# The last two experts in another order: both ups ahead of both downs, with the turns and the rows inside the downs

## The reference

```
h = rmsnorm(x, g);  proj = h @ w_in                 # q, k, v, pooling input, gates
... pooling branch, attention branch ...
x = x + merged @ w_out
h2 = rmsnorm(x, ffn_g)
logits = h2 @ router_w + router_b;  top_v, top_i = lax.top_k(logits, 4);  top_p = softmax(top_v)
for e in range(32):
    g = min(t @ w_gate[e] + b_gate[e], 7)
    u = clip(t @ w_up[e] + b_up[e], -7, 7)
    act = (u + 1) * (g * sigmoid(1.702 * g))
    out = out + comb[:, e:e+1] * (act @ w_down[e] + b_down[e])
```

## Time and profile before

| | us |
|---|---|
| runs | 1078.42, 1079.12, 1079.86 |
| median | 1079.12 |
| profiled execution, its own time | 1078.32 |
| its span | 1076.0 |
| TensorE busy | 1046.0 (97%) |
| VectorE busy | 272.9 (25%) |
| ScalarE busy | 199.7 (19%) |
| DMA | 433.65 MB, mean 403 GB/s |

### The profile page before, as it was taken

One profiled execution on the slowest core, in us unless ns is written; L12 is line 12 of the kernel. 1 busy time (PEld: TensorE's weight loads), 2 busy tenths in 40 slices (PEclk: granted clock), 3 DMA queues, 4 the chain that ended last, 5 costly groups with the idle time before them and its releaser, 6 DMA issues.

```text
span 1076.0 us, 12286 instructions
## 1 busy us (share of the span) xinstructions
PE 1046.0 (97%) x5121; PEld 445.2 (41%) x5121; DVE 272.9 (25%) x548; ACT 199.7 (19%) x348; POOL 40.4 (4%) x55
## 2 busy tenths in 40 slices
PE   9999999999999999999999999999999999999997
PEld 5899984333333333333333333333333333333332
DVE  6876753111111111111111111111111011111121
ACT  4667522111111101111111111111111011111011
POOL 0460020000000000000000000000000000000000
PEclk9999999999999999999999999999999999999999
DMA  9835999999999999999999999999999999999997
GB/s 313 307 124 163 406 392 378 409 426 428 440 427 431 429 432 432 432 431 434 429 431 432 432 434 430 432 431 430 434 434 430 432 431 430 425 429 429 429 421 282
DMA packets 37947, 433.65 MB, mean 403 GB/s; under 512 B 5109, under 2 KB 7962, under 8 KB 20122
## 3 DMA queue, kind: packets, MB, share of 16 engines
q1 hardware_dynamic: 37280, 432.64, 95.9%
q10 hardware_dynamic: 634, 0.56, 0.2%
HBM read 432.14 MB, written 1.05 MB: 403 GB/s over the span
## 4 chain that ended last, share of the span: by engine, by line
PE 70%; DMA 25%; ACT 3%; DVE 1%; issue 0%; DVEq 0%
PE ps L1063 45%; DMA ring<-in_exp_w_up 22%; PE ps L951 4%; PE ps L691 4%; PE ps L692 4%; PE ps L693 4%; DMA arena<-in_exp_w_up 3%; PE ps L1011 3%; ACT arena L1382 2%; PE ps L1000 1%; PE ps L1071 1%; PE ps L757 1%; PE ps L819 0%; PE ps L968 0%; PE ps L705 0%; ACT ring_r L1244 0%
## 5 line engine op out<-in xcount | busy, mean ns | idle before, releaser
L1063 PE MATMUL ps<-ring,arena 128*64 128x512 f32 x2432 | 543.3, 599 | 12.4 <-DMA ring<-in_exp_w_up 12.1
L1063 PEld LDWEIGHTS ps<-ring,arena 128*64 128x64 f32 x2432 | 168.2, 137 | 337.0 <-issue 313.5
L1063 PE MATMUL ps<-arena 128*64 128x512 f32 x640 | 142.0, 595 | 2.1 <-DMA arena<-in_exp_w_up 1.9
L1880 DVE TENSOR_SCALAR arena<-ps 128x512 f32<-128x512 f32 x30 | 20.8, 692 | 464.4 <-PE ps L1063 464.4
L1382 ACT COPY arena<-ps 128x512 f32<-128x512 f32 x31 | 32.5, 1048 | 255.9 <-PE ps L951 255.9
L1063 PEld LDWEIGHTS ps<-arena 128*64 128x64 f32 x640 | 44.0, 137 | 86.5 <-issue 81.5
L1893 DVE TENSOR_SCALAR arena<-ps 128x512 f32<-128x512 f32 x31 | 21.4, 692 | 177.2 <-PE ps L1063 177.2
L1011 PE MATMUL ps<-arena 64*128 64x512 f32 x256 | 63.9, 616 | 0.0
L1422 ACT COPY arena<-ps 128x256 f32<-128x256 f32 x30 | 11.2, 372 | 279.3 <-PE ps L1011 279.3
L691 PE MATMUL ps<-ring_r 128*128 128x256 f32 (+1 forms) x192 | 59.1, 308 | 0.4 <-DVE arena_r L1682 0.3
L951 PE MATMUL ps<-arena 128*64 128x512 f32 x248 | 58.5, 592 | 0.0
(11 more groups left out here) (245 smaller groups left out, 673.0 us busy)
## 6 DMA issues: line engine op xcount, KB each, us to landing
ring<-in_exp_w_up SPq DMA_DIRECT2D x19, 4096.0 KB, 31.9
ring<-in_exp_w_down SPq DMA_DIRECT2D x18, 4096.0 KB, 31.3
ring<-in_exp_w_gate SPq DMA_DIRECT2D x18, 4096.0 KB, 32.5
ring<-in_exp_w_up SPq DMA_DIRECT2D x10, 2048.0 KB, 39.6
ring<-in_exp_w_down SPq DMA_DIRECT2D x10, 2048.0 KB, 38.9
ring<-in_exp_w_gate SPq DMA_DIRECT2D x10, 2048.0 KB, 40.3
arena<-in_exp_w_gate SPq DMA_DIRECT2D x5, 4096.0 KB, 32.5
arena<-in_exp_w_down SPq DMA_DIRECT2D x5, 4096.0 KB, 34.0
```

What stands on the lines that cost most here:

```text
L1063: last = mm(ps[BLOCK * to:BLOCK * (to + 1), bank, :], src[:, c, half, :], moved, start=(fresh and half == 0 and c == 0), stop=(half == 1 a ...
L1880: v.tensor_scalar(g1, ps[:, 4, :], LIMIT, None, ALU.min).then_inc(g_ready, 1)
```

## The change

Four things move.

The order of the last six matrices is now gate 30, up 30, gate 31, up 31, down 30, down 31, for the loads as for the products. Up 31 and down 30 are both loaded in four pieces of two chunks (up 31 had five, the last two of one chunk). The weights of the last rows are turned inside up 31, ahead of chunk 4. Expert 31's activation is turned inside down 30, ahead of chunks 3 and 5, and the rows of expert 30 are put back inside down 31, ahead of chunks 3 and 5. Down 31 goes to bank 5, since bank 7 is still being read.

The turn of the parameters and the spread of the norms are now two functions; the spread stands ahead of chunk 6 of the first query strip.

The second tile's `pick` for the first expert no longer reads `rank_tab`. It compares the sums in the accumulator directly, and is weighted with `chosen` times the norm; `rank` follows behind it.

```diff
-        GATE30, UP30, GATE31, DOWN30, UP31, DOWN31 = range(PAIR, PAIR + 6)
-        TAIL = {DOWN30: (0, 2, 4, 6, 8), UP31: (0, 2, 4, 6, 7, 8), DOWN31: (0, 2, 4, 6, 7, 8)}
+        GATE30, UP30, GATE31, UP31, DOWN30, DOWN31 = range(PAIR, PAIR + 6)
+        TAIL = {UP31: (0, 2, 4, 6, 8), DOWN30: (0, 2, 4, 6, 8), DOWN31: (0, 2, 4, 6, 7, 8)}
...
-            def spread_norm():
+            def turn_columns():
                 pe.wait_ge(rows_in, 16 * 4)
                 tr(ps[:, 1, R_BGATE:R_ROWS], prow[R_BGATE:R_ROWS, :],
                    ident[R_BGATE:R_ROWS, R_BGATE:R_ROWS]).then_inc(cols_T, 1)
+
+            def spread_norm():
                 pe.wait_ge(con_rest, 16)
...
                                 turn_x(1, 1)
+                                turn_columns()
+                            if t == 0 and c == 6:
                                 spread_norm()
...
-                product(r, 0, DOWN30, 7, actT, fresh=True)
-                pe.wait_ge(weights_ready, r + 1)
-                turn_weights(6)
...
                 pe.wait_ge(pickT_ready, i + 2)
                 biases(1, 5, next_e)
-                product(r, 0, UP31, 5, last_h_in)
-
-                pe.wait_ge(y_ready, i + 2)
-                scatter_tile(0, y_e, pickT)
-                pe.wait_ge(act_first, r + 1)
-                turn_part(0, 4).then_inc(turn_first, 1)
-                scatter_tile(1, y_e, pickT).then_inc(rows_down, 1)
-                pe.wait_ge(act_ready, i + 2)
-                pe.wait_ge(pickT_ready, i + 3)
-                turn_part(1, 6).then_inc(act_T, 1)
+                product(r, 0, UP31, 5, last_h_in, [(4, last_weights)])
+                pe.wait_ge(actT_ready, i + 1)
+                product(r, 0, DOWN30, 7, actT, [(3, first_turn), (5, second_turn)], fresh=True)
                 pe.wait_ge(actT_first, r + 1)
-
-                def rows_turned():
-                    pe.wait_ge(actT_ready, i + 2)
-
-                product(r, 0, DOWN31, 7, last_actT, [(2, rows_turned)], fresh=True)
+                product(r, 0, DOWN31, 5, last_actT, [(2, rows_turned), (3, first_rows), (5, second_rows)], fresh=True)
...
             dve.wait_ge(chosen_ready, 2)
+            own(v.tensor_tensor(first_weight, chosen[:, 1, 0:1], rstd[:, 1:2], ALU.mult))
             dve.wait_ge(rank_done, 2)
+            v.tensor_scalar(pick[:, 1, :], iota, ps[:, 2, 0:1], first_weight, ALU.is_equal, ALU.mult).then_inc(first_pick, 1)
             rank(1)
-            select_tile(1, 0).then_inc(first_pick, 1)
```

More of the change, by code:

```diff
@@ L248, in build @@
         ss_more = small[:, 186:187]
+        first_weight = small[:, 187:188]
         ss2 = small[:, 196:200].rearrange("p (t h) -> p t h", t=NT)
@@ L270, in build @@
         down30_in = [sem(f"down30_in{i}") for i in range(2)]
-        up31_in = [sem(f"up31_in{i}") for i in range(3)]
+        up31_in = [sem(f"up31_in{i}") for i in range(2)]
         down31_in = [sem(f"down31_in{i}") for i in range(5)]
@@ L473, in build @@
         FINE = E - 5
-        GATE30, UP30, GATE31, DOWN30, UP31, DOWN31 = range(PAIR, PAIR + 6)
-        TAIL = {DOWN30: (0, 2, 4, 6, 8), UP31: (0, 2, 4, 6, 7, 8), DOWN31: (0, 2, 4, 6, 7, 8)}
-        TAIL_IN = {DOWN30: [quarter_in[DOWN30 % HOLDS][0], down30_in[0], quarter_in[DOWN30 % HOLDS][1], down30_in[1]],
-                   UP31: [quarter_in[UP31 % HOLDS][0], up31_in[0], quarter_in[UP31 % HOLDS][1], up31_in[1], up31_in[2]],
-                   DOWN31: down31_in}
+        GATE30, UP30, GATE31, UP31, DOWN30, DOWN31 = range(PAIR, PAIR + 6)
+        TAIL = {UP31: (0, 2, 4, 6, 8), DOWN30: (0, 2, 4, 6, 8), DOWN31: (0, 2, 4, 6, 7, 8)}
+        TAIL_IN = {n: [quarter_in[n % HOLDS][0], seconds[0], quarter_in[n % HOLDS][1], seconds[1]]
+                   for n, seconds in ((UP31, up31_in), (DOWN30, down30_in))}
+        TAIL_IN[DOWN31] = down31_in
         def tail_count(signal, r):
@@ L495, in matrix @@
                 return divmod(n, MATRICES)
-            return ((E - 2, 0), (E - 2, 1), (E - 1, 0), (E - 2, 2), (E - 1, 1), (E - 1, 2))[n - PAIR]
+            return ((E - 2, 0), (E - 2, 1), (E - 1, 0), (E - 1, 1), (E - 2, 2), (E - 1, 2))[n - PAIR]
         h_split = tuple(ring_r[seat[H_SLOT]][:, NC * S * i:NC * S * (i + 1)].rearrange("p (c s) -> p c s", c=NC)
@@ L1147, in last_pair, with last_weights, first_turn, second_turn @@
                 product(r, 0, GATE31, 4, last_h_in, [(3, lambda: turn_results(i))])
-                pe.wait_ge(actT_ready, i + 1)
-                product(r, 0, DOWN30, 7, actT, fresh=True)
-                pe.wait_ge(weights_ready, r + 1)
-                turn_weights(6)
+                def last_weights():
+                    pe.wait_ge(weights_ready, r + 1)
+                    turn_weights(6)
+                def first_turn():
+                    pe.wait_ge(act_first, r + 1)
+                    turn_part(0, 4).then_inc(turn_first, 1)
+                def second_turn():
+                    pe.wait_ge(act_ready, i + 2)
+                    pe.wait_ge(pickT_ready, i + 3)
+                    turn_part(1, 6).then_inc(act_T, 1)
+                def first_rows():
+                    pe.wait_ge(y_ready, i + 2)
+                    scatter_tile(0, y_e, pickT)
+                def second_rows():
+                    scatter_tile(1, y_e, pickT).then_inc(rows_down, 1)
+                def rows_turned():
+                    pe.wait_ge(actT_ready, i + 2)
                 pe.wait_ge(pickT_ready, i + 2)
                 biases(1, 5, next_e)
-                product(r, 0, UP31, 5, last_h_in)
-                pe.wait_ge(y_ready, i + 2)
-                scatter_tile(0, y_e, pickT)
-                pe.wait_ge(act_first, r + 1)
-                turn_part(0, 4).then_inc(turn_first, 1)
-                scatter_tile(1, y_e, pickT).then_inc(rows_down, 1)
-                pe.wait_ge(act_ready, i + 2)
-                pe.wait_ge(pickT_ready, i + 3)
-                turn_part(1, 6).then_inc(act_T, 1)
+                product(r, 0, UP31, 5, last_h_in, [(4, last_weights)])
+                pe.wait_ge(actT_ready, i + 1)
+                product(r, 0, DOWN30, 7, actT, [(3, first_turn), (5, second_turn)], fresh=True)
                 pe.wait_ge(actT_first, r + 1)
-                def rows_turned():
-                    pe.wait_ge(actT_ready, i + 2)
-                product(r, 0, DOWN31, 7, last_actT, [(2, rows_turned)], fresh=True)
+                product(r, 0, DOWN31, 5, last_actT, [(2, rows_turned), (3, first_rows), (5, second_rows)], fresh=True)
                 def last_scatter(t, q):
@@ L1439, in last_pair @@
                 fn(sig, g1, ACT.Sigmoid, scale=ALPHA).then_inc(sig_ready, 1)
-                act.wait_ge(piece_done, pieces + 2 * (DOWN30 + 1))
-                nc.scalar.copy(y_e, ps[:, 7, :]).then_inc(y_ready, 1)
                 act.wait_ge(pick_T, i + 2)
@@ L1448, in last_pair @@
                 nc.scalar.copy(turned[:, 2 * P:], ps[:, 6, 2 * P:]).then_inc(actT_ready, 1)
+                act.wait_ge(piece_done, pieces + 2 * (DOWN30 + 1))
+                nc.scalar.copy(y_e, ps[:, 7, :]).then_inc(y_ready, 1)
                 act.wait_ge(piece_done, pieces + 2 * (DOWN31 + 1))
-                nc.scalar.copy(last_y[:, 0:HALF // 2], ps[:, 7, 0:HALF // 2]).then_inc(y_first, 1)
-                nc.scalar.copy(last_y[:, HALF // 2:], ps[:, 7, HALF // 2:]).then_inc(y_ready, 1)
+                nc.scalar.copy(last_y[:, 0:HALF // 2], ps[:, 5, 0:HALF // 2]).then_inc(y_first, 1)
+                nc.scalar.copy(last_y[:, HALF // 2:], ps[:, 5, HALF // 2:]).then_inc(y_ready, 1)
             def experts(r):
```

## The result

| | before | after |
|---|---|---|
| median us (runs) | 1078.95 (20) | 1080.13 (20) |
| lowest to highest | 1077.83 to 1080.78 | 1079.33 to 1081.77 |
| ratio, 95% interval | | 1.0013 [1.0007, 1.0018] |
| profiled execution: own time, span | 1078.32, 1076.0 | 1080.27, 1078.0 |

The change costs 1.4 us by the ratio (0.8 to 1.9 by the interval); the two medians are 1.2 apart. The forecast was 1080.3.

What follows compares the result with a forecast made beforehand. The weight stream was taken to set the end from about 700 us; tail +1.6, second pick -0.2 and spread 0 gave +1.4 us, set on the mean 1078.93: 1080.3 us, range for the time 1078.3 to 1081.6.

Steps and rivals of the forecast that it cites:

- The bound: From about 700 us the weight stream sets the kernel's end; work saved on TensorE comes back as longer waits.
- The tail, +1.6: Last down waits for pieces at 1059.6 and 1062.1, then 7.57 us of chunks and rows stand uncovered: 1.6 us later.
- The second pick, -0.2: Front, second tile: pick ready 0.23 us earlier, two keepers hold TensorE until about 169.8; -0.2 us, bounds -0.2 and 0.
- The spread of the norms, 0: Front: VectorE waits 0.75 us longer, but key strips hang on ScalarE's square; 0 us, bounds 0 and +0.75.
- (d): Front: VectorE's 0.75 us from the later spread pass into the front, giving 1081.1 us; chance 0.07.
- The sum: Whole kernel: +1.6 - 0.2 + 0 = +1.4 us, set on the mean 1078.93, giving 1080.3; chance 0.50.
- One of its signs of being wrong: End of stream: the prediction is wrong if the last landing moves by over 0.3 us against the first product.
- (a): Tail: landings don't bite and the last down runs through; tail -0.16 to +0.1, giving 1078.7 us; chance 0.27.
- (b): Tail: TensorE's waits are the price and landings follow the consumer; -1.7 - 0.2, giving 1077.0 us; chance 0.05.
- (c): Tail: the clock falls after a wait, behind 1062.1 where nothing covers it; 1.7 us on top, 1082.0; chance 0.11.

Runs made afterwards that it cites:

- e5: Kernel before with five more clock keepers (matmuls of no use) ahead of gate 30, where a wait for a landing follows; 1079.03 us, ratio 1.0002.
- e6: Kernel before with five more clock keepers ahead of down 31, where no wait is left; 1080.20 us, ratio 1.0012.
- e1: Kernel after with the old spread of the norms and the old pick, so the tail's change alone; 1080.21 us, ratio 1.0013.
- e3: Kernel after without the two tiles of rows of expert 30 inside the last down, leaving them out of the output; 1078.51 us, ratio 0.9992.
- e8: Kernel after with one clock keeper instead of two between the rank's sums and the second gather; one execution, 1081.55 us.
- e9: Kernel before with one clock keeper instead of two behind the counts of the ranks; one execution, 1078.92 us.
- e2: Kernel before with the late spread of the norms and the early second pick, so the front's change alone; 1078.67 us, ratio 0.9995.
- e4: Kernel after with down 31 loaded in six pieces, so that chunk 2 needs only half of the second; 1079.81 us, ratio 1.0008.
- e7: Kernel before with expert 30's rows moved into up 31, ahead of chunks 2 and 4; 1079.64 us, ratio 1.0005.

## Why the prediction was right, point by point

**The bound.** Right. The share stayed at 1.00 up to 1000 us, and e5 shows that 1.3 us of work on TensorE at 1014 us, ahead of waits, is free (1.0002), while e6 shows that behind the last wait it is paid in full.

**The tail, +1.6.** Right, by its own steps. The first piece was to land at 1059.6 and the second at 1062.1; in e1 it was 1059.33 and 1061.81, after 1060.08 and 1062.57, e3 1060.85 and 1063.33. The distance of 2.49 held in all of them (2.48, 2.49, 2.48), which is what the interpolation rested on; the level moves with the stream. Behind the second piece I had 7.57 us, counted as the old product was with 6.86; its row ends 0.23 later (7.09), so 7.80 to the end of the row. Measured 7.78. On the common measure the tail costs 1.62. That the rows are the uncovered work is shown by e3 (1.74 back in the trace, 1.7 in the time).

**The second pick, -0.2.** Wrong, and this is the step: "two clock keepers from 169.35 hold TensorE until about 169.8". A pair of keepers holds it until 0.67 us behind its start, 169.95 in the profile after: I had taken 0.23 for each of the two starts (0.73 less 0.50), but the gather behind the second one comes later than a second keeper does behind the first. In the earlier trace rows the gather at 170.01 follows the pick's end at 169.93 so closely that VectorE looked like the only cause. With one keeper (e8) the gather starts 0.44 us behind it and 0.07 behind the comparison's end, so there it follows the pick, as in e9, and the pick's 0.22 us show. The price of the scalar from the accumulator is now measured: 0.32 us against 0.31, and the old form took 0.32 too in e9.

**The spread of the norms, 0.** Right in its effect, off in one size: VectorE waits 1.14 us, not 0.75, and starts 1.0 later. The spread itself starts at 14.00, 1.86 later than the 12.14 of the earlier trace rows, where I had reckoned with two chunks of 0.86 and VectorE at 14.5. The slack of ScalarE's path held it, as said, and rival (d) fell: the key strips are not later, and e2 is not slower.

**The sum.** 1080.3 stood for +1.6 and -0.2; the runs gave 1080.13. By the terms as measured it would be +1.6 on the mean of 1078.93, 1080.5. That the median is 0.4 under this is inside the interval (0.8 to 1.9). So the mechanism and the size of the tail were right, but that the forecast came within 0.2 us is in part luck: the 0.2 wrongly taken off for the pick happens to make up half of those 0.4.

**One of its signs of being wrong came.** The prediction called itself wrong if the last landing moved by over 0.3 us against the first product. It did: in the trace's record of the landings it comes 894.15 us behind it in the kernel before and 894.62 after, 0.47 later, and the second piece of the last but one matrix moved alike, from 879.34 to 879.78. The change's order is not needed for that: in e1, with the same order of loads, the second piece comes after 879.06, earlier than before. The limit of 0.3 was narrower than the stream's scatter, so the sign could not tell anything. For the same reason the last down ends 2.08 us later from the start of the span and not 1.4: the stream's shift is some 0.4 of it.

**The rivals.** (a), landings that don't bite, fell: every trace of the new order has its waits inside down 31. (b) fell: the old waits were filled and the time rose, while the landings kept their distances (the last one 14.85 us behind the second piece before and 14.88 after, by the record of the landings). (c) did not occur in the changed kernel's profiled execution nor in e1, e3, e4 or e8. Its event is real, as e7 shows, and there it stood where nothing covered it; the longest wait of the changed kernel's tail on a matmul row is 0.64 us, and in e7 it was 1.17 and 0.46 close together. That is one case and no rule. Only one execution of each kernel has a trace: six of the changed kernel's 20 times lie from 1081.02 to 1081.77, and whether such a product or a late landing made them is not known. (d) fell as told. As to the section "Optimization Strategies" of "Perfetto Trace Analysis" in the Trainium skill, by which the matmul engine is to be kept going: here the change did the turns beside the waits of down 30 and lost, and e6 against e5 shows that what counts is what stands behind the last landing.

No kernel here is faster than the kernel before by more than can be told; e2's 0.9995 [0.9986, 1.0004] is the lowest that computes the whole output.

## What to carry to other kernels

Where a stream of loads sets the end, find the last landing that the program waits for, and add up the work that stands behind it: here only that was paid (e5 against e6). Small work (rows, turns) costs nothing ahead of the last waits only if it uncovers nothing elsewhere: e7 put the rows there and uncovered VectorE's activation. The new order with the rows in the two waits of down 31 was not run, so whether it could have been saved is not shown. Before pricing an earlier result at a gain, list everything that holds its consumer, on the consumer's own engine too; two holders that end together look like one in a trace.

## What the hardware showed that was not expected

- The stream's landings near the end moved between 1051.80 and 1053.60 us for the same transfer over the profiled executions, while the distances behind it stayed: down 31's first piece to its second is 2.49 within 0.02, and the last landing lies 14.85 to 14.96 behind the second piece (e4 aside). The front doesn't explain it: from the first product to this landing it is 879.34 us in the kernel before, 879.24 in e2, 879.78 after and 880.74 in e8. The record of the landings shows single late ones: the two halves of gate 31 each land 4.90 us behind the load ahead of them in the kernel before, but the first came 5.92 behind in the kernel after and 6.08 in e3, and the second 6.45 in e8. Why is open. All three are of the new order; e1 and e4, of the same order, have at most 5.11 there, so these traces don't tell whether the order has a part in it. The times leave little room for it: 1.4 us (0.8 to 1.9) against the tail's 1.62.
- A product at the lower granted clock costs 1.69 us (8.78 against 7.09) and yet delayed nothing where TensorE waits for the stream once an expert anyway: the waits of 1.7 us are as long as the loss. In the uncovered tail the same 1.69 us is paid in full (e7).
